# One-core two-block transformer step: mixers with their heads woven between half units of projections, and feed-forward and norms on a ring of 1 MB weight units, token tile by token tile

## The reference, cut to what matters

```python
# first_block, two layers:
h = rmsnorm(x, norm_mix_pre)
m = attention_mixer(h) if layer == 0 else recurrent_mixer(h)
x = x + rmsnorm(m, norm_mix_post)
f = swiglu(rmsnorm(x, norm_ffn_pre), w_gate, w_up, w_down)      # width 2816
x = x + rmsnorm(f, norm_ffn_post)
# second_block, two layers:
h = h + dilated_diff_mixer(rms_norm(h, attn_norm));  h = h + swiglu_2(rms_norm(h, ffn_norm))
h = h + hgrn2_mixer(rms_norm(h, hgrn_norm));         h = h + moe_swiglu(rms_norm(h, moe_norm))
# moe: 8 experts of width 3584, the two best for each token
```

## Time and profile before

| | us |
|---|---|
| median of three runs | 2329.12 (2326.53 to 2331.10) |
| the profiled execution's own time | 2333.04 |
| its span in the trace | 2331.3 |
| TensorE busy in it | 2191.8 (94%) |
| VectorE busy | 1424.3 (61%) |
| ScalarE busy | 1194.4 (51%) |

### The profile page before, as it was taken

How to read it: one execution, slowest core, us unless ns; L and a number is a source line. 1 busy time by engine, 2 the same in 40 slices (tenths; PEclk the granted TensorE clock), 3 DMA queues, 4 the chain that set the end, 5 groups by cost and what they waited for, 6 DMA issues and landing times.

```text
span 2331.3 us, 28572 instructions
## 1 busy us (share of the span) xinstructions
PE 2191.8 (94%) x11126; PEld 1797.8 (77%) x11126; DVE 1424.3 (61%) x1256; ACT 1194.4 (51%) x1148; POOL 36.3 (2%) x87
## 2 busy tenths in 40 slices
PE   7988998979998978999897899999999999999998
PEld 5647997759997646998764588888888888888887
DVE  1335543345434364543424488889888888888888
ACT  1344431534332153432734267777677777776775
POOL 2000000000000000000000000000000000000000
PEclk9998998989998979999997799999999999999999
DMA  8305546434554303565420299999999999999997
GB/s 309 109 0 172 180 162 211 141 118 150 175 208 144 109 0 109 176 203 216 145 73 19 104 361 347 363 351 356 355 354 372 339 371 342 368 343 363 350 360 267
DMA packets 216998, 535.76 MB, mean 230 GB/s; under 512 B 9469, under 2 KB 79262, under 8 KB 216942
## 3 DMA queue, kind: packets, MB, share of 16 engines
q1 hardware_dynamic: 213936, 530.61, 63.4%
q0 software_dynamic: 1088, 4.19, 0.5%
q10 hardware_dynamic: 1918, 0.18, 0.1%
HBM read 533.90 MB, written 1.05 MB: 229 GB/s over the span
## 4 chain that ended last, share of the span: by engine, by line
PE 84%; ACT 8%; DVE 5%; issue 2%; POOL 0%; DMA 0%; ACTq 0%; DVEq 0%; POOLq 0%
PE ps L1700 12%; PE ps L1702 12%; PE ps L1701 11%; PE ps L431 8%; PE ps L548 6%; PE ps L549 6%; PE ps L550 6%; PE ps L458 5%; PE ps L435 3%; ACT ring_r L1691 3%; PE ps L563 3%; PE ps L564 3%; PE ps L565 3%; PE ps L1710 1%; PE ps L1753 1%
## 5 line engine op out<-in xcount | busy, mean ns | idle before, releaser
L1696 DVE TENSOR_TENSOR ring_r<-ring,ring_r 128x2048 fp32r<-128x2048 f32 x339 | 761.7, 2287 | 92.7 <-ACT ring_r L1691 92.7
L1691 ACT ACTIVATE ring_r<-ring 128x2048 fp32r<-128x2048 f32 x339 | 629.1, 1910 | 36.3 <-DMA ring<-in_moe_w_gate 29.3
L1700 PE MATMUL ps<-ring_r,arena_r 128*128 128x512 f32 x1344 | 531.8, 396 | 1.0 <-DVE arena_r L1932 1.0
L1702 PE MATMUL ps<-ring_r,arena_r 128*128 128x512 f32 x1344 | 524.4, 390 | 0.0
L1701 PE MATMUL ps<-ring_r,arena_r 128*128 128x512 f32 x1344 | 524.2, 390 | 0.0
L1702 PEld LDWEIGHTS ps<-ring_r,arena_r 128*128 128x128 f32 x1344 | 252.7, 188 | 54.6
L1700 PEld LDWEIGHTS ps<-ring_r,arena_r 128*128 128x128 f32 x1344 | 252.8, 188 | 51.5 <-issue 1.1
L1701 PEld LDWEIGHTS ps<-ring_r,arena_r 128*128 128x128 f32 x1344 | 253.1, 188 | 50.4
L431 PE MATMUL ps<-arena,ring 128*128 128x256 f32 x1152 | 259.6, 387 | 7.4 <-DVE arena L374 5.3
L431 PEld LDWEIGHTS ps<-arena,ring 128*128 128x128 f32 x1152 | 223.2, 194 | 43.3 <-DVE arena L374 6.6
L549 PE MATMUL ps<-arena_r,ring_r 128*128 128x256 f32 x816 | 233.4, 286 | 0.0
(11 more groups left out here) (326 smaller groups left out, 2758.7 us busy)
## 6 DMA issues: line engine op xcount, KB each, us to landing
ring<-in_moe_w_gate SPq DMA_DIRECT2D x115, 1024.0 KB, 5.1
ring<-in_moe_w_up SPq DMA_DIRECT2D x112, 1024.0 KB, 5.1
ring<-in_moe_w_down SPq DMA_DIRECT2D x112, 1024.0 KB, 4.9
ring<-in_ffn_w_gate SPq DMA_DIRECT2D x33, 1024.0 KB, 7.3
ring<-in_ffn_w_up SPq DMA_DIRECT2D x33, 1024.0 KB, 9.7
ring<-in_ffn_w_down SPq DMA_DIRECT2D x33, 1024.0 KB, 5.0
ring<-in_attn_w_in SPq DMA_DIRECT2D x12, 2048.0 KB, 12.5
ring<-in_hgrn_w_in SPq DMA_DIRECT2D x8, 2048.0 KB, 9.8
```

What stands on the lines that cost most here:

```text
L1691: nc.scalar.activation(unit_parts(k)[0], ring[:, slot_of(k), 0:2048], ACT.Copy).then_inc(m_hi, 1)
L1696: nc.vector.tensor_tensor(low, ring[:, slot_of(k), 0:2048], high, ALU.subtract).then_inc(m_lo, 1)
L1700: nc.tensor.matmul(out_, x[:, 0, f, :], w[0], start=first, stop=False)
L1702: return nc.tensor.matmul(out_, x[:, 0, f, :], w[1], start=False, stop=last)
```

## The change

Feed-forward and mixers share one list of 1 MB units (`weights`) on the five slots. A slot holds the raw unit in its first half; a split unit's high part goes into the second half and its low part over the raw one. A slot is loaded again when the unit five before it in the list is used (`w_used`). Mixer units stay plain fp32 (`halves=False`). The feed-forward's loops are written out: gate, up, down of pairs of 128 columns, with `highs_to`/`lows_to` three units ahead. Each mixer's heads are put between half units (128 columns).

Norms: the gain is multiplied in the scaling (`gpre`, broadcast by GpSimd's queue); the pass over Y by the gain and the square with sum run beside each other in halves; HT is laid out by token tile (`HTf`, `HTh`, `HTl`). `first_tokens` starts a stage with tile 0 alone on three or four units, turns tile 1 before the last of them, then does tile 1. The output projections' tile 1 comes in a second pass over the four units, with tile 0's transposes before its last unit. R's tanh/ln/exp/sqrt chain becomes tanh (of half the argument) and sqrt in halves; G's functions are grouped.

```diff
+        def norm_scalar(act, k, early, late):
+            norm_sums(act, k, 0)
+            norm_high(act, k, 0)
+            highs_to(act, early)
+            norm_sums(act, k, 1)
+            highs_to(act, late)
+            norm_high(act, k, 1)
+        def norm_vector(dve, step, k, early, late):
+            if k:
+                residual(dve, step, k, 0)
+            normalise_tokens(dve, step, k, 0)
+            norm_low(dve, k, 0)
+            lows_to(dve, early)
+            if k:
+                residual(dve, step, k, 1)
+            normalise_tokens(dve, step, k, 1)
+            lows_to(dve, late)
+            norm_low(dve, k, 1)
+        def first_tokens(pe, k, pairs):
+            if k % 2 == 0:
+                pe.wait_ge(s_hth, 4 * k + 2)
+            pe.wait_ge(s_htl, 4 * k + 2)
+            for n, (u, bank, how) in enumerate(pairs):
+                if n == len(pairs) - 1:
+                    norm_turn(pe, k, 1)
+                weights_ready(pe, u)
+                how(pe, u, bank, ts=(0,))
...
+            for u, bank, how in pairs:
+                how(pe, u, bank, ts=(1,)).then_inc(w_used, 1)
+        def out_last_tokens(pe, plan, m, x, ns):
+            for n in ns:
+                if n == 3:
+                    norm_turn(pe, 2 * m + 1, 0)
+                out_tensor(pe, plan, m, x, n, 1)
@@ feed-forward, ahead = 3 @@
+            for what, i in order:
+                unit_ = {"g": g, "u": u, "d": d}[what][i]
+                highs_to(act, unit_ + ahead)
+                if what == "g":
+                    gated(i)
+                elif what == "u" and i != 0:
+                    high(0 if i == 1 else i)
@@ F_scalar: early and late are the first up unit @@
-            norm_scalar(act, norm_at_ffn[i])
-            ffn_norm_scalar(act, FFN[i], norm_at_ffn[i])
-            ffn_scalar(act, FFN[i])
+            norm_scalar(act, norm_at_ffn[i], FFN[i][1][0], FFN[i][1][0])
+            ffn_scalar(act, i, FFN[i], AHEAD_FF)
@@ A_tensor: weaving @@
+            for n in range(8):
+                half(4 + n // 2, n % 2)
+                scores(n)
+            half(8, 0)
+            turn(0)
+            scores(8)
+            for n in range(1, 8):
+                half(8 + n // 2, n % 2)
+                turn(n)
+                values(n - 1)
+                scores(8 + n)
@@ M_scalar; M_vector has split_low likewise ahead of residual @@
             for k in range(AHEAD):
                 split_high(act, 0, k)
-            norm_scalar(act, 7)
+            norm_sums(act, 7, 0)
+            norm_sums(act, 7, 1)
@@ sync @@
+            for u, (shape, src) in enumerate(weights):
+                if u >= NS_EARLY:
+                    sp.wait_ge(*used(u - NS_EARLY))
+                sp.dma_start(shape(slot_raw(u)), src).then_inc(landed[u % NS_EARLY], 16)
...
             for k in range(NU):
                 if k < NS_EARLY:
-                    sp.wait_ge(*freed[slot_of(k)])
+                    sp.wait_ge(*used(N1 - NS_EARLY + k))
```

More of the change, by code:

```diff
@@ L225, in slot_k, with unit @@
-        def slot_k(s):
-            return ring[:, s, :].rearrange("p (k n) -> p k n", k=KT)
-        def columns_of(w, c0, n=512):
-            return lambda s: [(slot_k(s)[:, :, 0:n], w.rearrange("(k p) n -> p k n", p=P)[:, :, c0:c0 + n])]
-        units = [0]
+        weights = []
+        split_no = []
+        def unit(shape, src, halves):
+            split_no.append(sum(n is not None for n in split_no) if halves else None)
+            weights.append((shape, src))
+            return len(weights) - 1
@@ L979, in A_vector @@
+            evac(11)
+            turned(7), output(3)
+            exps(3)
+            for n in range(8, 16):
+                turned(n)
+                if n % 2 == 0 and n > 8:
+                    output(n // 2 - 1)
+            highs_to(act, A_out[3][0] + 1)
+            output(7)
         def A_vector(dve, step):
-            norm_vector(dve, step, 0, between=lambda: columns_vector(dve, step))
-            distances_vector(dve, step)
-            params_vector(dve, step)
+            norm_vector(dve, step, 0, 0, 0)
@@ new lines, in E_scalar @@
+            for j in range(4):
+                evac(j)
+            root(0), root(1)
+            evac(4)
+            root(2)
+            evac(5)
+            root(3)
+            exps(0)
+            evac(6)
+            root(4)
+            exps(1)
+            turned(0)
+            evac(7)
+            output(0, 0)
+            root(5)
+            exps(2)
+            turned(1)
+            evac(8)
+            output(1, 0)
+            root(6)
+            exps(3)
+            turned(2)
@@ L1312, in E_scalar, with copies @@
+            root(7)
+            evac(9)
+            output(2, 0)
+            turned(3)
+            evac(10)
+            output(3, 0)
             squares(8)
+            exps(4)
             root(8)
-            act.wait_ge(e_qn, 9)
-            first_split_scalar(act, FFN[2])
+            evac(11)
+            def copies(x):
+                for n in range(4):
+                    if n < 3:
+                        turned(heads_before(x) + n)
+                    if n:
+                        output(x, n - 1)
@@ L1482, in exps @@
+            evac_q(2)
+            evac_q(3)
+            for u in range(4):
+                act.wait_ge(s_evac, G_evac(4 + u))
+                ins = nc.scalar.activation(pair(G_q, u), pair(G_q, u), ACT.Silu)
+            ins.then_inc(g_silu, 1)
             def exps(h):
@@ new lines, in G_scalar @@
+            exps(0)
+            exps(1)
+            evac(8)
+            for i in range(HG + 2):
+                if i % 2:
+                    evac(9 + i // 2)
+                if i < HG:
+                    keys(i)
+                if i + 2 < HG:
+                    exps(i + 2)
+                if i >= 2:
+                    output(i - 2)
+                    if i % 2:
+                        u = i // 2 - 1
+                        act.wait_ge(g_oc, 2 * u + 2)
+                        nc.scalar.activation(G_sq[:, u, :], pair(G_o, u), ACT.Square).then_inc(g_sq, 1)
@@ L1656, in build @@
             sem("m_" + n) for n in ("sel", "ga", "xh", "xl", "tr", "st", "sct", "sc", "yh", "yl"))
[L1657 removed]
+        M_n0 = [16 * len(range(s, N1, NS_EARLY)) for s in range(NS_EARLY)] + [0, 0]
         GATE_U, UP_U, DOWN_U = range(3)
```

1846 lines of the change are left out of this document (939 added, 907 removed).

## The result

The changed kernel takes 2248.34 us (median of 4 runs, 2247.92 to 2249.88) against 2328.02 (4 runs): ratio 0.9657, interval 0.9641 to 0.9674. That is 79.7 us less where 91.2 were forecast; the time, 10.3 above the predicted 2238, lies in the range. In the two profiled executions the spans differ by 2331.3 - 2245.9 = 85.4 us; the prediction's sum said 91.2.

The account below looks back on a forecast made before the run. TensorE, busy 94% of the span, bounds the kernel; its idle and low-clock time in mixers, gaps and start could be won. 68.8 + 25.4 + 2.0 - 9.9 + 4.9 = 91.2 us off 2329.1 gives 2237.9, said as 2238; range 2208 to 2270.

Parts of the forecast that it names:

- rival 4: Feed-forwards: the five 1 MB slots starve them of weights, making the kernel slower, over 2329 us; chance 0.03.
- The mixers: All four mixers, stripped of idle and low-clock time with remaining waits added: 68.8 us less, bounds 34 and 81.7.
- Rival 1: Mixers: heads stay paced by VectorE and ScalarE, so half the mixers' gain goes, 2272 us; chance 0.20.
- A: First mixer: from 159.6 us to a floor of 144.9 plus waits and split units, 152.0; 7.6 less.
- G: Last mixer, before stage M: from 198.2 us to a floor of 169.1, with a 1 us stall 171.0; 27.2 less.
- R: Second mixer: from 109.2 us to a floor of 99.9, plus 1.4 behind the last gate unit, 102.0; 7.2 less.
- E: Third mixer: from 186.1 us to a floor of 153.7, plus 4 us of stalls and other costs, 159.3; 26.8 less.
- Into a mixer: Gaps before the three later mixers: token-tile split hides norm relays, leaving 3.8, 3.8 and 2.0 us; 25.4 less in all.
- Into a feed-forward: Feed-forward entries: 3.5 us idle at tile 1's transposes, 4.8 before the second gate unit; net gain 2.0 over three.
- Into M: Entry of stage M: expert splits ahead of tile 0's norm leave TensorE 10.4 us idle; net 9.9 us lost.
- The start: Before the first matmul: gain multiplications go and x comes in halves, so 11.5 us instead of 16.45; 4.9 less.
- Rival 3: Stage starts: TensorE's clock falls, costing 4 us at each of three mixers, 12 in all, 2250 us; chance 0.12.

Follow-up runs that it names:

- whole-unit run: Changed kernel with R, E and G turning tile 1 directly behind tile 0 and starting on whole 256-column units instead of tile 0's half first: 2279.84 us.

## Why the prediction was right, and where its sizes were off

- **What bounds the kernel**: right. The loop of M kept its 1002 us, the feed-forwards were not starved (rival 4; no weight load is among TensorE's waits but the first of all), and nearly all the gain came from the mixers and the gaps.
- **The mixers**, -64.5 against -68.8: right in sum, with errors of both signs that cancel, which is luck. Where TensorE has units to put under the heads the waits went: idle before the last quarter is 0 in R and 0.05 in G. Rival 1 (half the gain) is out by these 64.5 us, and undoing the weave costs E and G 25.5 and 39.2, although its cause shows in E, where VectorE and ScalarE still hold TensorE for some 6 us (under the 10 that the prediction named as the sign of being wrong).
- **A** is the step that failed: "Floor 144.9" took the busy time of before as fixed. Its 13.5 us of idle fell to 5.3, but busy time grew from 146.1 to 153.6. The heads' scores went from 12.6 us (most heads side by side in pairs) to 17.3 (one by one); pairs give 6.3 us back, of 6.9 missing (7.6 - 0.7). In the 6.3 is a part of what the joints cost: a half unit takes 3.66 us between two heads, and 3.50 as a quarter of an unbroken run before. Besides, the last quarter ran at the low clock (5.29 us instead of 3.60), tile 1's transposes (0.9) stood in no term, and the slow phase at the start costs 1.6 (12.56 against 10.96 with TensorE warmed). With these the pieces come to 10.5 and not 6.9: the floor was also too high, by the step named next under G. Its 16 us at low clock held 2.5 of work, while the products from 16.45 to 20.45 us alone were 4 us of work at a granted clock of 0.50. The waits of 1.2 and 3.61 us at A's end had been priced at 1.7 and 3.6.
- **G** gained 6 us more than said. The error is in the step "a mean of c means that a share 2(1-c) of the time was at 1.2 GHz; what of it was not idle would take half as long". I took all idle time as low-clock time, and so too little of the work. The heads' small products took 35.6 us busy before and 27.5 after, with the same count; together with the output (30.2 to 28.3) and value units (30.1 to 29.0) that is 11.1 us and not 6.5. The forecast stall of 1 us did not come either.
- **R** gained 2.7 more than said and came out 0.6 below its own floor (99.3 against 99.9): the 1.4 us behind the last gate unit did not come, and the floor was too high, as in G. How much of the low clock it missed was not separated.
- **E** gained 6 us less: 6.2 us idle where 4 were priced (2.2), its first 4 us of products at a clock of 0.57 (1.6 lost), the first output quarter at the low clock behind a wait (4.97 us instead of 3.60), and tile 1's transposes (0.9). These make 6.1; whether the joints cost as in A and the floor was off as in G, against each other, was not separated.
- **Into a mixer**: 3.8, 3.7 and 1.9 us against 3.8, 3.8 and 2.0; the seams of R and E show the walked pieces, 1.58, 1.31, 0.90. The whole-unit run shows that the split by tile carries it.
- **Into a feed-forward**: the 4.8 us in front of the second gate unit are there three times (14.4), as are their cause and their releaser. At tile 1's transposes 1.27 and 2.43 us and no wait at all stood where 3.5 were forecast.
- **Into M**: 10.05 us against 10.4, the releaser as named, and removable.
- **The start** was mis-sized: 4.9 against 0.7. The words "I take the first matmul at 11.5" priced the gain and left out the bias table and the post-norm gain, 2 MB that load at the same time; without them ahead of it the unit landed in time for 13.57, 2.2 us earlier. The other 2 us are the norm of tile 0: its transposes come at 10.34, and with them (1.94) and the copy (0.90) no first matmul could come before 13.2 us in this kernel.
- **Rival 3**, the clock at each start: 1.6 us in E, none in R and in G in this profile, not 12. In other profiles R's first half units took up to 1.6 us more as well, and E's none. The pauses there are 1.6 and 0.9 us; behind 7.6 us the whole-unit run has the low clock for most of 8 us.
- **Slips in the sums**: each mixer has sixteen more transposes inside it than before, not eight; those of tile 1 (0.9 in each of four) were left out, and R's sum left out the other eight as well. The four floors together lie 85.5 us under before, not 81.7. And rival 1's own time, 2272, lies outside the range that was said to take in most of it.
- **Against the medians**: the profiled execution of before was 2333.04 and lay 3.9 above its median, that of after 2247.92, 0.4 below. I carried the 3.9 over. So 6.1 us of the miss of 10.4 are in the sum (91.2 against 2333.04 - 2247.92 = 85.1), 4.3 in this, which has nothing to do with the change.

## What to carry to other kernels

Before small products are moved between large ones, look in the timeline whether they overlap each other where they stand: a pair that runs side by side should move as a pair. Price an engine's queue at a seam by walking it in issue order; every split or copy that waits for a late slot belongs behind the work that the slow engine is waiting for, and the four such places (three gate units, M) were worth 22.9 us here. When a mean clock is turned into lost time, count the instructions at each rate, do not assume that the low clock fell on the idle time.

## What the runs showed of the hardware

- At the start of the changed kernel 21 instructions ran in 4 us and then 38, with the granted clock at 1.00 in both windows; with 40 transposes ahead of them it was 36 in the first 4 us. In the kernel before the first products ran at a granted clock of 0.50 for 4 us and of 0.59 for the next 2. So the column can miss such a phase; the count of instructions in a stretch does not.
- Forty transposes of the identity ahead of the first products did as much for the rate as forty products (10.96 us for the next 96 in both). In the prediction the Trainium skill (TensorE: Matmul & The Clock Gate, Part 4: PE-mode transpose) stood for the contrary; for fp32 transposes of 128 by 128 no run here bears it out. In these two executions the transposes themselves reached the full rate later than the products: from 2 to 8 us there were 11, 11 and 13 of them in each 2 us, against 10, 12 and 17 instructions of products.
- A pause of 1.6 us with eight transposes and 0.9 us behind it left the clock up at R and lowered it at E in the same execution, and left it up at E in the run with 40 products. At G, with the 0.9 us alone, it stayed up; 7.6 us lowered it both times.
